# Transformer layer on one core: the second query group's projection joins the first stage, in halves that share a bank with the modulation sums

## What is computed

```python
cond = jax.nn.silu(c)
mod = cond @ mod_w[i] + mod_b[i]
sh_m, sc_m, gt_m, sh_f, sc_f, gt_f = jnp.split(mod[:, None, :], 6, axis=-1)
h = rms_norm(x, norm_g[i, 0]) * (1.0 + sc_m) + sh_m
y = swa_sink_attention(h, swa_w_qkv[j], swa_w_o[j], swa_sinks[j], cos, sin)
x = x + gt_m * rms_norm(y, norm_g[i, 1])
h = rms_norm(x, norm_g[i, 2]) * (1.0 + sc_f) + sh_f
x = x + gt_f * rms_norm(swiglu(h, ffn_w_in[i], ffn_w_out[i]), norm_g[i, 3])
```

## Time and profile before

| | us |
|---|---|
| median of 3 runs | 1133.84 |
| lowest and highest | 1131.18, 1135.58 |
| the profiled execution's own time | 1133.45 |
| its span in the trace | 1131.7 |
| last product of the output projection starts | 374.40 |

### The profile page before, as it was taken

How to read it: one execution, slowest core, us unless ns; L and a number is a source line. 1 busy time by engine, 2 the same in 40 slices (tenths; PEclk the granted TensorE clock), 3 DMA queues, 4 the chain that set the end, 5 groups by cost and what they waited for, 6 DMA issues and landing times.

```text
span 1131.7 us, 13640 instructions
## 1 busy us (share of the span) xinstructions
PE 1068.3 (94%) x4968; PEld 847.3 (75%) x4968; DVE 687.1 (61%) x870; ACT 485.6 (43%) x619; POOL 29.3 (3%) x39
## 2 busy tenths in 40 slices
PE   5788899899998799999999999999999999999996
PEld 2555766577786688888888888888888888888885
DVE  2686776878887836676675444445443545544456
ACT  4322456546763653333333433333334444334443
POOL 0000000000010100000000000000001000000000
PEclk9899999999998899999999999999999999999999
DMA  9999999988896426787785555555555455555542
GB/s 364 416 417 417 418 371 384 409 348 290 317 359 259 149 97 258 278 312 279 261 315 208 186 186 201 189 186 199 185 186 186 153 201 202 187 185 190 199 167 74
DMA packets 50599, 288.23 MB, mean 255 GB/s; under 512 B 6401, under 2 KB 6401, under 8 KB 23937
## 3 DMA queue, kind: packets, MB, share of 16 engines
q1 hardware_dynamic: 47090, 268.47, 63.4%
q0 software_dynamic: 2304, 16.78, 3.7%
q10 hardware_dynamic: 1168, 2.49, 0.6%
HBM read 285.36 MB, written 2.10 MB: 254 GB/s over the span
## 4 chain that ended last, share of the span: by engine, by line
PE 78%; DVE 9%; DMA 7%; ACT 3%; issue 3%; SPq 0%; POOL 0%; DVEq 0%; ACTq 0%; POOLq 0%
PE ps L1290 24%; PE ps L1292 24%; PE ps L1291 24%; DMA mraw<-in_mod_w 4%; DMA graw<-in_mod_h 3%; PE ps L1313 3%; DVE mraw L746 3%; DVE wlo L735 2%; ACT whi L396 2%; PE ps L1347 1%; PE ps L1447 1%; PE ps L1323 1%; PE ps L1336 0%; DVE wlo_in L735 0%; DVE guT L1155 0%
## 5 line engine op out<-in xcount | busy, mean ns | idle before, releaser
L735 DVE TENSOR_TENSOR wlo<-raw,whi 128x1024 fp32r<-128x1024 f32 x336 | 396.4, 1221 | 311.8 <-ACT whi L396 311.6
L1290 PE MATMUL ps<-whi,hThi 128*128 128x512 f32 x1232 | 489.5, 397 | 22.5 <-DVE wlo L735 18.5
L396 ACT ACTIVATE whi<-raw 128x2048 fp32r<-128x2048 f32 x168 | 321.5, 1915 | 396.5 <-PE ps L1292 381.5
L1291 PE MATMUL ps<-wlo,hThi 128*128 128x512 f32 x1232 | 483.9, 393 | 0.0
L1292 PE MATMUL ps<-whi,hTlo 128*128 128x512 f32 x1232 | 483.4, 392 | 0.0
L1290 PEld LDWEIGHTS ps<-whi,hThi 128*128 128x128 f32 x1232 | 233.8, 190 | 88.6 <-issue 36.1
L1292 PEld LDWEIGHTS ps<-whi,hTlo 128*128 128x128 f32 x1232 | 233.9, 190 | 49.7
L1291 PEld LDWEIGHTS ps<-wlo,hThi 128*128 128x128 f32 x1232 | 234.2, 190 | 47.5
L746 DVE CUSTOM_DVE_ANT_0 mraw<-mraw,cb,mbias 128x1024 f32<-128x1024 f32 x64 | 82.5, 1304 | 49.9 <-DMA mraw<-in_mod_w 49.9
L746 DVE CUSTOM_DVE_ANT_0 mraw<-mraw,cb,modT 128x1024 f32<-128x1024 f32 x64 | 81.4, 1282 | 21.8 <-DMA mraw<-in_mod_w 21.8
L1290 PE MATMUL ps<-whi,oThi 128*128 128x512 f32 x112 | 46.7, 417 | 6.6 <-DVE wlo L735 6.6
(11 more groups left out here) (151 smaller groups left out, 530.3 us busy)
## 6 DMA issues: line engine op xcount, KB each, us to landing
raw<-in_w_in SPq DMA_DIRECT2D x88, 1024.0 KB, 4.8
mraw<-in_mod_w SPq DMA_DIRECT2D x128, 512.0 KB, 8.0
raw<-in_w_out SPq DMA_DIRECT2D x44, 1024.0 KB, 4.8
raw<-in_w_qkv SPq DMA_DIRECT2D x24, 1024.0 KB, 11.8
graw<-in_mod_h SPq DMA_DIRECT2D x16, 1024.0 KB, 14.3
graw<-in_mod_h POOLq DMA_DIRECT2D x16, 1024.0 KB, 8.9
raw<-in_w_o SPq DMA_DIRECT2D x16, 1024.0 KB, 7.0
x<-in_x ACTq DMA_DIRECT2D x2, 1024.0 KB, 8.9
```

The costliest lines, as they stand in the source:

```text
L396: A(split_of(q, s)[0], raw[:, s], ACT.Copy).then_inc(hi_done, 1)
L735: V.tensor_tensor(low[:, k], raw[:, s, k], high[:, k].bitcast(F32), ALU.subtract).then_inc(done, 1)
L1290: mm(dst, hi, high[:, n], start=start, stop=False)
L1291: mm(dst, hi, low[:, n], start=False, stop=False)
```

## The change

The first stage's quarter gets a fourth block: keys, first query group, values, second query group, in this order (`load_first_w`), so that the joint projection's blocks 12 to 15 of before are done inside the quarters, and the stage's blocks are 0 to 15. Since no two banks are free for it, the fourth block of quarter c is done by halves in one bank (`last_q`): tokens 0 to 127 into bank 6 + c%2 (the one that this quarter's sums don't use), ScalarE copies it out (`q1_part`), then tokens 128 to 255 into the same bank, copied out again. The partial results of quarters 0 to 2 go to `q1a`, `q1b`, `q1c`, and VectorE adds them; in the last quarter the two halves take banks 6 and 7 and are added from there (`q1_total`).

```diff
+            def q1_part(c, b):
+                if b == 0:
+                    act.wait_ge(q1_pe, c + 1)
+                else:
+                    act.wait_ge(pe_done, 4 * c + 4)
+                A((q1a, q1b, q1c)[c][:, b], ps[:, 6 + c % 2], ACT.Copy).then_inc(q1_evac, 1)
...
             sums_out(0)
+            hi(0, 0)
             for c in range(4):
                 act.wait_ge(hf_done, c + 1)
                 A(hThi[:, 4 * c:4 * c + 4], nT[:, 4 * c:4 * c + 4], ACT.Copy).then_inc(hhi_done, 1)
-                for g in range(3 * c, 3 * c + 3):
-                    hi(g // 4, g % 4)
-                if c < 3:
-                    sums_out(c + 1)
+                hi(c, 1)
...
+                if c < 3:
+                    hi(c, 2)
+                    hi(c, 3)
+                    q1_part(c, 0)
+                    sums_out(c + 1)
+                    hi(c + 1, 0)
+                    q1_part(c, 1)
...
             for c in range(4):
                 modulate(c)
+                lo(c, 0, (0,))
                 h_lo(c)
-                lo_of(3 * c)
+                lo(c, 0, (1,))
+                if c == 0:
+                    angles()
...
+            def last_q(c, b):
+                if b == 0 and c == 3:
+                    pe.wait_ge(q1_evac, 6)
+                elif b and c < 3:
+                    pe.wait_ge(q1_evac, 2 * c + 1)
+                for t in range(WP):
+                    if b == 0 and t % 2 == 0:
+                        split_ready(c, 3, t // 2)
+                    k = WP * c + t
+                    last = three(ps[:, 6 + (b if c == 3 else c % 2)], hThi[:, k, b * P:(b + 1) * P],
+                                 hTlo[:, k, b * P:(b + 1) * P], c, 3, t, t == 0, t == WP - 1)
+                last.then_inc(pe_done if b else q1_pe, 1)
+
             for c in range(4):
                 pe.wait_ge(h_ready, c + 1)
...
+                project(c, c, hThi, hTlo, 0, half_done, slot=0)
+                if c < 3:
+                    sums(c + 1, (0,))
+                project(c, c, hThi, hTlo, 2, half_done, slot=1)
+                if c < 3:
+                    sums(c + 1, (1,))
+                    project(c, c, hThi, hTlo, 4, half_done, slot=2, halves=(0,))
+                    sums(c + 1, (2,))
+                    last_q(c, 0)
+                    sums(c + 1, (3,))
+                    project(c, c, hThi, hTlo, 4, half_done, slot=2, halves=(1,))
+                    columns(c + 1)
+                    last_q(c, 1)
...
+            project(3, 3, hThi, hTlo, 4, half_done, slot=2, halves=(0,))
+            k_turn()
+            project(3, 3, hThi, hTlo, 4, half_done, slot=2, halves=(1,))
+            last_q(3, 0)
+            q_turn(0)
+            last_q(3, 1)
+            scores(0)
+            q_block(16, (0,))
             gate_sums(16)
```

More of the change, by code:

```diff
@@ L556, in copy_y @@
+            oT_out(1)
+            hi_of(24)
+            probs(2, 0)
+            evac_q(3, 0)
+            sums_out(6)
+            probs(2, 1)
+            evac_q(3, 1)
+            hi_of(25)
+            normalise(2, 0)
+            normalise(2, 1)
+            hi_of(26)
+            sums_out(7)
             def copy_y(w, bank):
@@ L728, in _, with lo @@
             V = nc.vector
-            def lo(q, s):
-                dve.wait_ge(hi_done, 4 * q + s + 1)
+            def lo(q, s, parts=(0, 1)):
+                if 0 in parts:
+                    dve.wait_ge(hi_done, 4 * q + s + 1)
                 high, low = split_of(q, s)
-                for k, done in ((slice(0, 2), lo_half), (slice(2, 4), lo_done)):
+                for part in parts:
+                    k, done = ((slice(0, 2), lo_half), (slice(2, 4), lo_done))[part]
                     V.tensor_tensor(low[:, k], raw[:, s, k], high[:, k].bitcast(F32),
```

476 lines of the change are left out of this document (233 added, 243 removed).

## The result

| | median, us | range, us | runs |
|---|---|---|---|
| before | 1133.27 | 1128.05 to 1135.58 | 8 |
| after | 1144.68 | 1135.54 to 1148.76 | 8 |
| after, measured a second time | 1141.49 | 1137.96 to 1145.53 | 6 |
| before, beside it | 1131.31 | 1130.07 to 1135.85 | 11 |

The ratio after/before is 1.0091, 95% interval 1.0053 to 1.0128; in the second measurement 1.0075 (1.0052 to 1.0097). So the change costs 8 to 10 us, where no change was forecast, and both medians lie above the range given, the second by half a microsecond. The executions of the changed kernel also scatter over 13 us, and the one profiled first took 1135.54 us, the shortest of all. The second measurement's profile is of an execution of 1145.53 us (span 1143.7), 4 us above the median of its six, called the long execution; both are needed.

The account below looks back on a forecast made before the run. DMA and VectorE were taken to set the pace at the first part's end, TensorE in its middle; -8.5 us at the last scores and +7.8 in the output projection gave -0.7, so 1132.7 us, range 1125 to 1141.

Parts of the forecast that it names:

- Start of quarter 0: First stage: high part made earlier and `hTlo` last, so the quarter starts at 38.2, 1.8 us sooner.
- Quarters 0 to 2: First stage: 24 more products and two more stream breaks each, 6.1 us a quarter, 18.4 for three; quarter 3 at 137.6.
- The gaps: Ahead of quarters 1 to 3: 3.06 us idle each, 9.2 against 11.75 before, so 2.6 us won.
- The third rival: First stage becomes bound by DMA, each quarter taking its bytes' time: 1139 us in the middle, chance 0.04.
- The gate's waits: Quarter 3 to last scores: sums 18, 23 and 28 wait 0.8 to 2.4 us each, 4.8 in all, ends 0 and 7.2.
- The last scores: End of the scores at 272.0: 137.6 + 129.6 + 4.8, 8.5 us ahead of before.
- The output projection: Behind the scores: put-off passes' weights land late, 22.0 MB to pass 89 at 338.5, block 38 at 355.5; +7.8 us.
- The slower rival: Output projection: passes put off hold the end, 340 GB/s, 64.8 us, pass 89 at 346.5; 1140.7 us, chance 0.18.
- From pass 89 to block 38: Output projection: 12.9 us before, plus 3.6 for three more passes and 0.5 for late weights: 17.0.
- The sum's form: Whole kernel: last scores at -8.5 us, +7.8 given back in the output projection, -0.7 in all.

Follow-up runs that it names:

- act_order: Changed kernel with the copy of a quarter's second `q1` half moved behind the next quarter's `hThi` on ScalarE: 1141.81 us, ratio 1.0079 to the kernel before.
- small_after: Changed kernel with mod_w's pieces 34 to 95 cut to a quarter of their columns in load and VectorE pass: 1111.77 us, ratio 0.9819 to the kernel before.
- before_late: Kernel before with its passes and their loads put off by one to six places from pass 38, made up from 77 on: 1139.54 us, ratio 1.0064.
- the light pair: Changed kernel and kernel before, both with only the loads of mod_w's pieces 34 to 95 cut to a quarter: 1124.73 and 1124.81 us.
- the small pair: Changed kernel and kernel before, both with loads and VectorE passes of mod_w's pieces 34 to 95 cut to a quarter: 1111.77 and 1114.45 us.
- the two mends: Changed kernel with second `q1` half copied behind next `hThi` and passes forward from 39: 1137.74 us; with two more slots for gate pieces too: 1136.33 us.

## Why the prediction was wrong, point by point

- **Start of quarter 0** 38.2: 37.89. Right.
- **Quarters 0 to 2**, +6.1 us each, pitch 33: 32.9, then 30.8 and 30.8 us in the short execution, 32.4 for the third in the long one. Quarter 3 began at 132.43 (134.07), not 137.6. The term of 6.1 us was right; what was off is the clock, which I had left as it was. Quarter 2 of before, of the short and of the long execution:

```profile
96.04:123.55 27.51, 23.54 (x112) 16.05 (x113) 19.57 (x30) 5.76 (x5) 1.29 (x2) 0.94 1.02 417
```
```profile
101.61:132.43 30.82, 27.92 (x137) 19.17 (x137) 23.16 (x33) 10.30 (x9) 1.29 (x2) 1.00 1.02 417
```
```profile
101.64:134.07 32.43, 29.54 (x136) 20.30 (x137) 22.88 (x33) 10.27 (x9) 1.29 (x2) 0.94 1.02 419
```

At full clock TensorE is busy for 27.92 us; with one stretch of half clock (0.94) for 29.54, 1.6 us more. Before had such a stretch too: 23.54 - 1.6 = 21.9, and 27.92 is 6.0 more than that. Before had a stretch at the head of every quarter, the short execution only in quarter 0, so some 4 of the 5.2 us by which quarter 3 came early are clock, and the rest the gaps and the start. That is luck of the execution; the long one got less of it.
- **The gaps** of 3.06 us with `hThi` behind the last copy of `q1`: 2.89 each. Right in mechanism and size, and of little weight: act_order halved two of the three, and won 1 to 3 us at quarter 3 and nothing in the end.
- **The third rival** (first stage bound by the transfers) did not come about in the changed kernel. The DMA engines were full (1.02), but a quarter is TensorE's 27.92 us and the gap of 2.89: 30.81. Inside the quarters TensorE waited for nothing longer than 0.4 us, the quarter with half clock was longer by what TensorE was busy longer (32.43 and 30.82, 29.54 and 27.92), and in act_order a quarter with the same bytes took 29.38 us, less than the 30.2 that its 12.6 MB cost at 417 GB/s. The transfers come right behind, as that run's 5.18 us show. The Trainium skill, "DMA: Bandwidth & Descriptors", section Specifications, has some 358 GB/s for a core. The trace held 417 again over 84 us, so the 35.1 us a quarter, an estimate by this figure, did not come.

```profile
69.34:98.72 29.38, 27.92 (x137) 19.17 (x137) 21.96 (x34) 10.42 (x9) 0.00 (x0) 1.00 1.02 416
```

- **The gate's waits**, 4.8 us with 7.2 as an end: 7.1 us in the short execution, 8.0 in the long one. Too small, and they came at nine or five sums, not at three.
- **The last scores** at 272.0: 267.0 and 275.5. That the forecast lies between them is partly luck: from quarter 3 on it had 134.4 us, the short execution took 134.6 with longer waits and no half clock, the long one 141.4. Of the 8.5 us between the two executions some 7 are clock (the half-clock stretches behind 103, 134, 216 and 252 us, which the short one does not have).
- **The output projection** is the step that failed. I let 22.0 MB move from block 32's load to pass 89 at a rate between 374 and 417 GB/s and had pass 89 at 338.5, 66.5 us behind the scores. It took 73.9 and 75.8, and the +7.8 us of this part came as +14.7 and +17.1. Block 32's load was issued at 276.04, earlier than the 281.7 forecast, and pass 89 began 64.9 us later: 339 GB/s of what I had counted, where 56.8 us and so 387 were forecast. In the long execution the load came at 284.49 and pass 89 66.8 us later. The window itself moved 360 GB/s, 23.4 MB: pieces issued before it were still to land, 1.4 MB that the sum did not have (some 3.6 us at 387 GB/s, an estimate), and the rest of the 8.1 us is the lower rate.

```profile
276.04:340.90 64.86, 56.06 (x255) 44.17 (x253) 52.69 (x74) 35.07 (x65) 5.01 (x2) 0.92 0.96 360
```

- **The slower rival** said 340 GB/s, 64.8 us and 1140.7 us, at a chance of 0.18. It is what happened, in mechanism, in length (64.9 us) and nearly in the time (1141.5 and 1144.7). Its 346.5 for the start of pass 89 neither execution met (340.90 and 351.25), since they came to the scores 8.5 us apart; that its time is so near is in part luck. I held against it that the stretch begins sooner. What the profile had to say for it: a rate taken from a stretch with 25 passes behind the scores is no rate for one with 37. Each pass needs its piece and one of four slots, and each low part that TensorE wants stands behind the passes on VectorE. The sum had VectorE working with hardly a wait; it waited 12.1 us for pieces from 280 to 345. And it had no wait of TensorE ahead of pass 89, where there were 2.87 us at 293.70 and 5.62 at 306.69. The second, in rows: the high part of that block was made from 291.37 on; on VectorE six passes, one of them 2.05 us late, and `oT_lo` stood ahead of its low part.

```profile
291.37 1.90 ACT L392 ACTIVATE whi<-raw 128x2048 fp32r<-128x2048 f32 x1
...
302.76 1.29 DVE L772 CUSTOM_DVE_ANT_0 mraw<-mraw,cb,modT 128x1024 f32<-128x1024 f32 x1 [2.05 <-DMA mraw<-in_mod_w]
...
305.33 2.35 DVE L761 TENSOR_TENSOR wlo<-raw,whi 128x1024 fp32r<-128x1024 f32 x2
```

- **From pass 89 to block 38**, 17.0: 17.09 and 17.05. Right.
- **The sum's form** was wrong too. It took the lead at the last scores for a gain. But up to 200 us the changed kernel has moved 3.3 MB less, and has started four passes fewer: it does attention's work sooner and owes bytes and passes. TensorE's real gain is some 3.6 us, by small_after. Against it stand the passes put off, which cost before_late 7 us. The two don't add up: 8 to 10 us lost in spite of a gain of 3.6 are 12 to 14, and 5 to 7 of these are beyond what before_late shows.

What is shown: the 8 to 10 us go with the bytes (the light pair), and VectorE's passes are the next limit (the small pair); passes that come late are enough to cost 7 us; the best places for them and the two mends win 3 to 5 us of it back. What is ruled out as the one cause: the clock at the quarter starts, the copy ahead of `hThi`, the gate's slots, the two rotations. Earlier sums of the gate didn't help either, in an execution with other delays. What stays open is why the transfers are at 0.84 or 0.81 from 140 to 200 us, which order would fill them without a loss elsewhere, and where the 5 to 7 us beyond the late passes lie.

## What to carry to other kernels

A lead at one mark of the program is only a gain if, at that mark, the other engines and the transfers have done as much as before: compare bytes moved, passes done and blocks done at the same time, not only TensorE's position. Where the transfers are full for most of a stage, idle time of theirs is what a reordering costs, and it is paid for later, at the rate of the place where it is paid. And when the price of a stretch is its bytes over a rate, the rate must come from a stretch with the same mixture of work per byte; two rates at hand (374 and 340 here) are the ends of the range, and here the one from the stretch with more waiting was the right one. Compare executions at like clock before a lead is put down to the order: two profiles of one kernel stood 8.5 us apart at the same mark, some 7 of them clock.

## What the runs showed of the hardware

Behind idle gaps of like length the granted clock falls to half (1.2 GHz) in one execution and stays full (2.4 GHz) in the next. The gap of 2.89 us ahead of quarter 3 left the first product at 0.50 us in the short execution and at 0.80 in the long one; of 14 executions the mean clock ran from 0.972 to 0.984 and the time from 1148.8 to 1135.5 us. The Trainium skill, "TensorE: Matmul & The Clock Gate", Part 1, says that the number of slow products at a kernel's start varies from run to run for the same kernel. Here the same holds behind gaps in the kernel's middle. Over these runs the time scattered by about 1%, tied to the clock. So one profiled execution, above all the shortest of eight, is no picture of the median: the short one, at 1135.5 us against the kernel before's median of 1133.3, hid 9 of the 11 us between the medians.
